# Sliding-window attention: scores of the next head pairs ahead of the values of the last, and softmax ahead of the low part

## The reference, cut to what matters

```
q = (h @ w_q).reshape(B, NB, BLOCK, SWA_KV_HEADS, SWA_GROUP, SWA_HEAD_DIM)
s = einsum('bnqhgd,bnkhd->bnhgqk', q, kb) * (SWA_HEAD_DIM ** -0.5)
s = where(mask, s + bias, NEG)
m = maximum(max(s, axis=-1), sink)
p = exp(s - m)
p = p / (sum(p, axis=-1) + exp(sink - m))
o = einsum('bnhgqk,bnkhd->bnqhgd', p, vb)
return o.reshape(B, T, SWA_Q_HEADS * SWA_HEAD_DIM) @ w_out
```

## Time and profile before

| what | value |
|---|---|
| median of 3 runs | 969.11 us (969.1 to 969.15) |
| the profiled execution's own time | 970.28 us |
| its span | 968.5 us |
| TensorE (PE) busy | 959.9 us, 99% |
| TensorE's weight loads (PEld) busy | 829.1 us, 86% |
| VectorE (DVE) busy | 658.1 us, 68% |
| ScalarE (ACT) busy | 492.8 us, 51% |
| GpSimd (POOL) busy | 59.0 us, 6% |
| granted clock of TensorE | 0.998 |

### The profile page before, as it was taken

The page is one execution under the profiler, slowest core; times in us unless marked ns, Lnnn a source line. Parts: engine busy times, 40 slices in busy tenths (PEclk is TensorE's granted clock), DMA queues, the critical chain, the costliest instruction groups (busy, mean ns, idle before and its releaser), DMA issues.

```text
span 968.5 us, 13078 instructions
## 1 busy us (share of the span) xinstructions
PE 959.9 (99%) x5366; PEld 829.1 (86%) x5366; DVE 658.1 (68%) x930; ACT 492.8 (51%) x593; POOL 59.0 (6%) x129
## 2 busy tenths in 40 slices
PE   9999999999999999999999999999999999999997
PEld 9888888888889888888888889988888888888886
DVE  5877776555578977656666659767766765666665
ACT  5465554444448855544444445465554544444454
POOL 2441000000001001000000013000000000000000
PEclk9999999999999999999999999999999999999999
DMA  8663667677462335767765546453266465555551
GB/s 246 212 204 134 202 177 234 213 199 238 174 215 90 100 125 191 219 202 213 198 216 205 187 156 219 142 185 130 74 237 201 153 217 176 199 189 183 190 192 54
DMA packets 115251, 176.57 MB, mean 182 GB/s; under 512 B 5548, under 2 KB 78200, under 8 KB 115192
## 3 DMA queue, kind: packets, MB, share of 16 engines
q1 hardware_dynamic: 115016, 175.54, 56.1%
q10 hardware_dynamic: 176, 0.20, 0.1%
HBM read 174.03 MB, written 1.70 MB: 181 GB/s over the span
## 4 chain that ended last, share of the span: by engine, by line
PE 98%; DVE 1%; DMA 0%; ACT 0%; issue 0%; SPq 0%; DVEq 0%; ACTq 0%
PE ps L386 94%; PE ps L390 3%; DMA x<-in_x 0%; DVE M L1256 0%; DVE M L1264 0%; ACT M L2170 0%; DVE cc L1741 0%; DVE wlo L1256 0%; ACT M L2173 0%; SPq L2985 0%; DVE M L2150 0%; DVE cc L1740 0%; DVE x L1256 0%; DVE cc L1256 0%; ACT cc L2170 0%
## 5 line engine op out<-in xcount | busy, mean ns | idle before, releaser
L386 PE MATMUL ps<-whi,RR 128*128 128x512 f32 (+1 forms) x1556 | 397.5, 387 | 0.0
L1256 DVE TENSOR_TENSOR wlo<-raw,whi 128x1024 fp32r<-128x1024 f32 (+1 forms) x323 | 373.0, 1197 | 27.2 <-ACT whi L2173 27.0
L2173 ACT ACTIVATE whi<-raw 128x2048 fp32r<-128x2048 f32 (+1 forms) x161 | 301.3, 1873 | 164.0 <-PE ps L386 136.8
L386 PEld LDWEIGHTS ps<-whi,RR 128*128 128x128 f32 x1556 | 283.8, 188 | 55.4 <-issue 0.7
L386 PE MATMUL ps<-RR,whi 128*128 128x512 f32 (+1 forms) x1264 | 261.8, 351 | 0.0
L386 PEld LDWEIGHTS ps<-RR,whi 128*128 128x128 f32 x1264 | 201.5, 191 | 26.5 <-issue 1.3
L386 PE MATMUL ps<-wlo,RR 128*128 128x512 f32 (+1 forms) x778 | 220.5, 385 | 0.0
L386 PEld LDWEIGHTS ps<-wlo,RR 128*128 128x128 f32 x778 | 144.2, 188 | 29.4 <-DVE wlo L1256 0.2
L1256 DVE TENSOR_TENSOR M<-M,ps 128x512 f32<-128x512 f32 (+1 forms) x57 | 38.7, 682 | 172.6 <-ACT M L2173 168.3
L386 PEld LDWEIGHTS ps<-RR,wlo 128*128 128x128 f32 x1016 | 138.3, 191 | 9.1 <-DVE wlo L1256 0.7
L386 PE MATMUL ps<-RR,wlo 128*128 128x256 f32 x1016 | 144.7, 283 | 0.0
(11 more groups left out here) (109 smaller groups left out, 420.8 us busy)
## 6 DMA issues: line engine op xcount, KB each, us to landing
raw<-in_w_up SPq DMA_DIRECT2D x32, 1024.0 KB, 6.2
raw<-in_w_down SPq DMA_DIRECT2D x32, 1024.0 KB, 5.2
raw<-in_w_ff SPq DMA_DIRECT2D x32, 1024.0 KB, 5.1
raw<-in_w_in SPq DMA_DIRECT2D x23, 1024.0 KB, 5.0
raw<-in_a_w_in SPq DMA_DIRECT2D x10, 1024.0 KB, 5.5
raw<-in_a_w_out SPq DMA_DIRECT2D x4, 1024.0 KB, 5.1
raw<-in_b_w_q SPq DMA_DIRECT2D x4, 1024.0 KB, 5.4
raw<-in_b_w_out SPq DMA_DIRECT2D x4, 1024.0 KB, 5.1
```

Source lines behind the costliest of these rows:

```text
L386: return pe.matmul(out, lhsT, rhs, start=start, stop=stop, skip_group_check=True)
L1256: return dve.tensor_tensor(out, a, b, op)
L2173: return act.activation(out, in_, ACT.Copy, **k)
```

## The change

In TensorE's `window()`, `scores(i)` and `scores(i + 1)` are placed ahead of `values(i - 4)` and `values(i - 3)`. Where both are issued, that is for i = 4 and i = 6, the order changes. In VectorE's `window()`, the two `soft` of a turn are placed ahead of the turn's `lows`. Where both are issued, that is for a = 2 and a = 3, the order changes. In both, `shares` stays behind. ScalarE's, GpSimd's and SyncE's programs stay as they are.

```
@@ TensorE, window() @@
             if i < 10:
                 turned(i - 2)
+            if i % 2 == 0 and i < 8:
+                scores(i)
+                scores(i + 1)
             if i % 2 == 0 and i > 2:
                 values(i - 4)
                 values(i - 3)
-            if i % 2 == 0 and i < 8:
-                scores(i)
-                scores(i + 1)
@@ VectorE, window() @@
         for a in range(6):
+            if a < 4:
+                soft(2 * a)
+                soft(2 * a + 1)
             if a > 1:
                 lows(2 * a - 4)
             if a > 3:
                 lows(2 * a - 3)
             if a < 4:
-                soft(2 * a)
-                soft(2 * a + 1)
                 shares(2 * a)
             yield
```

## The result

The changed kernel takes 974.32 us (median of 6 runs, 972.66 to 975.92) against 969.13 us for the kernel before (6 runs, 969.06 to 970.39). The medians lie 5.2 us apart, where I had forecast 1.0. The ratio is 1.0047, with a 95% interval of 1.0038 to 1.0057, which is 3.7 to 5.5 us: slower, clear of the noise.

What follows compares the result with a forecast made beforehand. TensorE, busy without slack from 316 us on, was taken to bound the kernel, with VectorE next. Waits of 0.96 + 0.05 + 0 = 1.0 us on the median of 969.11 gave 970.1 us, range 969.0 to 971.0.

Steps and rivals of the forecast that it cites:

- The second turn: lows(2), bank 5, projection tile ("pr", 0, 1): TensorE, already 0.96 us late, would wait only 0 to 0.12 us more.
- the second term: TensorE's added wait for lows(2) at bank 5 in the projection: 0 to 0.12 us, taken as 0.05.
- I charge nothing for the clock: TensorE's granted clock was to stay at 1.00 despite the new waits, costing 0 us.
- VectorE's order in the first turn: soft(4) and soft(5) start 0.6 us earlier at 327.61; lows(0) ends 4.6 us later; shares(4) starts unchanged at 332.81.
- First term: TensorE's products of q(7) wait for lows(0) to empty bank 4, from 331.98 to 332.94: 0.96 us.
- Order of mode changes on TensorE: Gaps around swapped scores and values: three mode changes in either order, -0.16 to +0.16 us per turn, taken as 0.
- ScalarE: Later values delay highs and exps: exps(4) at 330.81 to 330.97, exps(6) at 342.11 to 342.27, shares(6) about a microsecond late.
- Third term: turned(6) on TensorE needs the delayed shares(6), with 0.2 us of margin left: 0, up to 0.1 us in the range.
- Nothing behind the stage takes up the loss: TensorE is busy in full for the 600 us behind the attention, so a microsecond lost there is paid at the end.
- Rival A: Waits at banks 4 and 5 add, as late exps(4) delays shares(4) by 0.9 us: 2.1 us, 971.2 us; chance 0.10.
- Rivals B and C: Former: bank 4 wait doesn't bind, 969.1 us, chance 0.10. Latter: earlier softs win 0.6 us per turn, 967.9, chance 0.05.

Runs made afterwards that it cites:

- the first turn alone: Both reorderings, TensorE's and VectorE's, kept only for i = 4 and a = 2, against the kernel before: 970.10 us, ratio 1.0013.
- second turn alone: Both reorderings, TensorE's and VectorE's, kept only for i = 6 and a = 3, against the kernel before: 975.37 us, ratio 1.0058.
- VectorE's half: Only VectorE's softs moved ahead of lows in both turns, TensorE's order as in the kernel before: 976.63 us, ratio 1.0076.

## Why the prediction was wrong

**The step that failed is "The second turn".** It says: "The same trade is made with lows(2), bank 5 and the tile ("pr", 0, 1) of the projection, which TensorE takes at 342.20", and so "the second wait is covered by the first". I had asked only who takes the bank that lows(2) empties. But `lows` has two kinds of followers: the next to take the bank, and whoever reads what it writes. In `projection()` stands `lambda k: K.empty(pv_tile(k))`: before each k, TensorE waits for the `lows` of that pair's tile, and k = 2, the third of ("pr", 0, 0), reads what lows(2) writes. TensorE wants it at 339.59, 2.6 us before it takes bank 5. lows(2) had ended at 337.92 + 0.69 = 338.61 in the kernel before, a microsecond ahead of that, and was put back to 343.69 - 0.61 = 343.08. With this reader, the prediction's own time for lows(2) with the semaphore, 343.15, gives 343.15 - 339.59 = 3.56 us for both waits together; 3.55 were measured. So the second term, put at 0.05 us, was 2.66.

**"I charge nothing for the clock" failed as well**, as a consequence. It rested on a wait of 1.3 us. After one of 2.71 us the clock did fall, and that cost 1.5 us more. With 0.89 for the first wait and 2.66 for the second this makes the 5.02 us.

The other steps held, each less the 0.61 us of start:

- VectorE's order in the first turn: lows(0) predicted to end at 332.90, measured 332.74 + 0.68 - 0.61 = 332.81.
- First term, 0.96 us for q(7) at bank 4: 0.89, by the first turn alone 0.88.
- Order of mode changes on TensorE, -0.16 to +0.16 us per turn, taken as 0: the gaps are 0.17, 0.33 and 0.17, in sum 0.67 as before, and the kernel with the new order in the first turn and no wait is 0.01 us off. The gap of 0.33 goes with the scores and moved with them. The Trainium skill, TensorEngine Tiling (Array Packing), Key Properties, says that a change of tiling mode drains TensorE; both orders have three changes, and the trace agrees in that the three gaps come to 0.67 us in either.
- ScalarE: exps(4) at 330.81 to 330.97, measured 331.50 - 0.61 = 330.89; exps(6) at 342.11 to 342.27, measured 342.69 - 0.61 = 342.08. shares(6) a microsecond late: 344.66 - 0.61 = 344.05, with 0.97 us of idle time before it.
- Third term, 0: turned(6) never waited. But TensorE came so much later than I thought that the 0.2 us of margin was not put to the test, so this says little for the reckoning.
- Nothing behind the stage takes up the loss: the offset stays to the end. The span is 5.7 us longer, which is 5.02 and the 0.61 of the start.

Rival A had two waits and was nearer in size, by a mechanism that did not occur (shares(4) did not slip by 0.9 us), and priced at 2.1. Rivals B and C are refuted by the waits and by the +0.88 and -0.01 us of the first turn.

## What to carry to other kernels

When an instruction is moved back on an engine, list everyone who waits for its semaphore: the next owner of the buffer that it frees and every reader of what it writes, each with the time at which it wants it, and let the earliest decide. On a saturated engine two delays don't add if both go back to one late event elsewhere; the last arrival counts, so testing the turns one by one shows more than halving the change. A wait on TensorE is not priced by its length alone: one that is longer than any after which the trace still shows the full clock may cost more than itself.

## What the hardware showed that I had not expected

Waits before weight loads of 0.56, 0.73, 0.86, 1.17, 1.26 and 1.32 us left the granted clock at 1.00 in the traces here. After those of 2.71 us (changed kernel) and 3.51 us (second turn alone) it fell to 0.50, and each time this cost 1.5 us: 5.02 - 3.55, and 4.94 less the 27.36 - 23.88 = 3.48 us lost at the wait. In the changed kernel it did not fall during the wait but with TensorE at work again since 343.75: the window to 345 us still has 1.00, the next 0.56. With 3.96 us of waiting (VectorE's half) it fell just ahead of the wait's end at 344.93, since the window from 343 to 345 us has 0.91. Not each run of the changed kernel seems to have paid for it: the time of the fastest is that of the waits alone, though no trace shows that execution. The Trainium skill, TensorE: Matmul & The Clock Gate, HAM oscillation — how this bites in real kernels, says that a wait in which TensorE has nothing to do can throttle it, so that the work behind it starts at half clock. The trace agrees with the fall, 0.50 from 346 to 348 us, but not with where it begins: up to 345 us the work behind the wait still had 1.00. With useless products in the wait the clock was 1.00 in the profiled execution, and the length 1.66 us less.
